# Sample states and SSD output projection of a decoder step: two blocks merged into one

## What is computed

```python
# per sequence; h is the state [group 4, head-in-group 8, 64, 128]; cum = cumsum(dt * a_neg)
y = y + einsum('blgn,bgjpn->blgjp', cc, h) * exp(cum)[..., None]      # read of the carried state
h = h * exp(last)[..., None, None] + einsum('bsgn,bsgjp->bgjpn', bc, xdt * w_s)   # its update
...
y = y + d_skip * xs
gated = y * silu(z)                                                    # [tokens, 2048]
gated = gated * rsqrt(mean(gated**2 over each of 4 groups of 512) + 1e-6)
mixer_out = (gated * norm_w) @ w_out                                   # w_out [2048, 1024]
```

## Time and profile before

| | |
|---|---|
| median of 3 runs | 1516.48 us (1514.39 to 1521.14) |
| the profiled execution, its own time | 1507.41 us |
| its span, first to last instruction | 1505.6 us |
| granted TensorE clock, mean | 0.849 of 2.4 GHz |
| TensorE matmul busy | 1281.0 us (85%) |
| VectorE busy | 459.2 us (31%) |
| ScalarE busy | 240.7 us (16%) |
| GpSimd busy | 131.3 us (9%) |

### The profile page before, as it was taken

How to read it: one execution, slowest core, us unless ns; L and a number is a source line. 1 busy time by engine, 2 the same in 40 slices (tenths; PEclk the granted TensorE clock), 3 DMA queues, 4 the chain that set the end, 5 groups by cost and what they waited for, 6 DMA issues and landing times. The chain is left out here.

```text
span 1505.6 us, 14743 instructions
## 1 busy us (share of the span) xinstructions
PE 1281.0 (85%) x5148; PEld 696.3 (46%) x5148; DVE 459.2 (31%) x1209; ACT 240.7 (16%) x570; POOL 131.3 (9%) x191
## 2 busy tenths in 40 slices
PE   7999946678996999999888489779998989998881
PEld 4777744466663335333333245545565353333330
DVE  0057745442435005322211432222110054122114
ACT  0101122110002003111111312321111032111111
POOL 0000012421000000111110000000000001111100
PEclk9999978655556998999999699597766989999996
DMA  5333450002322247799998540423524277999983
GB/s 231 120 112 111 174 226 0 29 1 83 113 111 102 84 168 287 273 424 422 423 422 368 213 201 0 132 58 96 141 79 188 91 290 295 426 423 422 424 341 114
DMA packets 54798, 309.34 MB, mean 205 GB/s; under 512 B 12818, under 2 KB 17810, under 8 KB 33362
## 3 DMA queue, kind: packets, MB, share of 16 engines
q1 hardware_dynamic: 44786, 295.42, 49.7%
q0 software_dynamic: 9216, 10.51, 2.0%
q10 hardware_dynamic: 736, 2.62, 0.6%
HBM read 300.61 MB, written 30.97 MB: 220 GB/s over the span
## 5 line engine op out<-in xcount | busy, mean ns | idle before, releaser
L1098 PE MATMUL ps<-ring,xsT 128*64 128x512 f32 x704 | 165.7, 625 | 28.1 <-DMA ring<-in_experts 23.6
L302 PE MATMUL ps<-XT,ring 128*128 128x320 f32 x640 | 175.4, 438 | 11.2 <-DMA ring<-in_w_in 11.2
L302 PEld LDWEIGHTS ps<-XT,ring 128*128 128x128 f32 x640 | 123.2, 193 | 62.9 <-issue 13.2
L1098 PEld LDWEIGHTS ps<-ring,xsT 128*64 128x64 f32 x704 | 56.7, 143 | 134.2 <-issue 127.7
L1420 DVE TENSOR_TENSOR work<-work,ps 128x256 f32<-128x256 f32 x32 | 13.5, 420 | 271.7 <-ACT work L1178 271.7
L822 PE MATMUL ps<-ring,zT 128*128 128x512 f32 (+1 forms) x192 | 87.8, 605 | 0.0
L1125 PE MATMUL ps<-ring,hT 128*64 128x512 f32 x352 | 80.4, 598 | 2.2 <-DVE hT L1425 1.7
L1098 PE MATMUL ps<-hi,xsT 128*64 128x512 f32 x320 | 70.9, 595 | 5.5 <-DMA hi<-in_experts 5.5
L1024 PE MATMUL ps<-C 128*128 128x512 f32 x124 | 68.8, 672 | 0.0
L1230 POOL DMA_INDIRECT y_dram<-ys,index x32 | 32.2, 1007 | 377.5 <-DVE ys L1431 377.5
L1222 POOL DMA_INDIRECT XT<-x_dram,index x32 | 32.7, 1020 | 351.4 <-DVE index L1366 319.7
(11 more groups left out here) (292 smaller groups left out, 1657.1 us busy)
## 6 DMA issues: line engine op xcount, KB each, us to landing
ring<-in_experts SPq DMA_DIRECT2D x40, 2048.0 KB, 25.9
ring<-in_experts SPq DMA_DIRECT2D x52, 1024.0 KB, 24.6
hi<-in_experts SPq DMA_DIRECT2D x20, 2048.0 KB, 25.7
ring<-in_w_in SPq DMA_DIRECT2D x10, 2048.0 KB, 7.7
hi<-in_experts SPq DMA_DIRECT2D x20, 1024.0 KB, 31.0
ring<-in_latent SPq DMA_DIRECT2D x48, 256.0 KB, 2.9
ring<-in_w_out SPq DMA_DIRECT2D x4, 2048.0 KB, 12.8
ring<-in_state SPq DMA_DIRECT2D x4, 1024.0 KB, 6.9
```

What stands on the lines that cost most here:

```text
L302: mm = pe.matmul(ps[:, q, 0:TOK], ring[:, u, k * 512 + q * P:k * 512 + (q + 1) * P], XT[:, k, :], start=(k == 0), stop=(k == KD - 1))
L1098: mm = pe.matmul(ps[e * SLOTS:(e + 1) * SLOTS, GU[p], :].rearrange("p (g f) -> p g f", g=2), xsT[:, p, k, e * SLOTS:(e + 1) * SLOTS], w[:, ...
```

## The change

`sample_states` and `out_projection` become one block, `states_and_output`.

- Samples are taken in four pairs: sample i of the first half and sample i of the second, so that a pair has rows 0 to 31 and rows 32 to 63 of the 64. States are loaded and stored in that order.
- State read: C, zeroed outside its own sample, is the stationary operand (32 columns) and the state moves (512 columns). The four groups write four 32-partition strips of one PSUM bank; the samples of a half accumulate. exp(cum) is applied afterwards on VectorE (`ecS`), the result is transposed (`turn_reads`) and added to `xbcT`. Chunk 2 no longer makes exp(cum) per unit on ScalarE nor the product on GpSimd.
- State update: one matmul for each sample of a pair and group, with 32 rows, on row strips 0 and 32 of the array, into banks 6 and 7.
- Norm and projection of the 256 prompt columns start at once, without the samples; an update of a pair and group stands between two channel blocks. The sample rows have their own norm and are projected last, the two column halves of the output on the two halves of the PSUM partitions; ScalarE copies one half to its place.
- `wout_used` is set by the sample rows' matmuls, so by the last part of the block. SP issues the state outputs of the last pair before the first expert.

```diff
-                            for b in range(4):
-                                sp.dma_start(h0[b], a["state"][b]).then_inc(state_in[b], 16)
+                            for b, n in enumerate((0, 4, 1, 5)):
+                                sp.dma_start(h0[b], a["state"][n]).then_inc(state_in[b], 16)
...
                     for u in range(UNITS):
-                        if c:
+                        if carried:
                             act.wait_ge(seg_in, u + 1)
...
+                @block.sync
+                def _(sp):
                     load_router(sp, 0)
                     for i in range(4):
+                        if i == 3:
+                            sp.wait_ge(y_turned, 1)
+                            sp.dma_start(lnp[:, :, :], a["ln"][0]).then_inc(ln_in, 16)
+                        for half in range(2):
+                            n, b = batch(i, half)
+                            sp.wait_ge(updated, 8 * i + 7 + half)
+                            sp.dma_start(o["ssds"][n], h0[b]).then_inc(state_out, 16)
+                        if i < 2:
+                            sp.wait_ge(state_out, 32 * (i + 1))
+                            for half in range(2):
+                                n, b = batch(i + 2, half)
+                                sp.dma_start(h0[b], a["state"][n]).then_inc(state_in[b], 16)
+                        if i == 2:
+                            sp.wait_ge(state_out, 32 * (i + 1))
+                            sp.dma_start(X[:, :, :], a["x"]).then_inc(x_in, 16)
+                    sp.wait_ge(wout_used, 1)
+                    first_expert(sp, 0, 0)
+                    sp.wait_ge(wout_used, 2)
+                    first_expert(sp, 0, 1)
+                    sp.wait_ge(state_out, 128)
+                    sp.wait_ge(wout_used, 3)
+                    first_expert(sp, 0, 2)
+                    sp.wait_ge(wout_used, 4)
+                    first_expert(sp, 0, 3)
...
+                    def read_states(i):
+                        for half in range(2):
+                            n, b = batch(i, half)
+                            pe.wait_ge(state_in[b], 16 * (i // 2 + 1))
+                            for g in range(GROUPS):
+                                mm = pe.matmul(ps[32 * g:32 * g + 32, YB[half], :], Cm[:, g, half, 32 * i:32 * i + 32],
+                                               h0[b][:, g * 512:(g + 1) * 512], start=(i == 0), stop=(i == 3))
+                            mm.then_inc(read_done, 1)
...
+                    def prompts(blk):
                         pe.wait_ge(wout_in[blk // 4], 16)
                         pe.wait_ge(scaled, blk + 1)
+                        at = (blk % 4) * D
+                        for t in range(2):
                             for n in range(2):
+                                pe.matmul(ps[:, 2 * t + n, :], zT[:, blk, OFF[t]:OFF[t] + P],
+                                          ring[:, blk // 4, at + n * 512:at + (n + 1) * 512], start=(blk == 0), stop=(blk == ZB - 1))
+
+                    def update(i, g):
+                        if i or g:
+                            pe.wait_ge(updated, 8 * i + 2 * g)
+                        for half in range(2):
+                            rows = slice(32 * half, 32 * half + 32)
+                            pe.matmul(ps[:, UP[half], :], Bm[rows, i, g * STATE:(g + 1) * STATE],
+                                      xdtw[rows, g * 512:(g + 1) * 512], start=True, stop=True).then_inc(up_done, 1)
...
+                    def samples(blk):
+                        pe.wait_ge(scaled_s, blk + 1)
+                        at = (blk % 4) * D
+                        for n in range(2):
+                            mm = pe.matmul(ps[64 * n:64 * n + 64, SB, :], zT[:, blk, SAMPLE],
+                                           ring[:, blk // 4, at + n * 512:at + (n + 1) * 512], start=(blk == 0), stop=(blk == ZB - 1))
                         if blk % 4 == 3:
                             mm.then_inc(wout_used, 1)
...
+                    for g in range(GROUPS):
+                        squares(g)
+                    pe.wait_ge(masked, GROUPS)
+                    pe.wait_ge(ec_done, 1)
+                    read_states(0)
+                    read_states(1)
+                    for blk in range(ZB):
+                        if blk % 4 == 0 and blk >= 8:
+                            read_states(blk // 4)
+                        prompts(blk)
+                        if blk == 0:
+                            pe.wait_ge(std_done, GROUPS)
+                            pe.wait_ge(bm_done, 4)
+                        if blk < 12:
+                            update(*divmod(blk, 4))
+                        elif blk == 12:
+                            turn_reads()
+                        elif blk < 15:
+                            update(3, blk - 13)
+                    sample_squares()
+                    update(3, 2)
+                    for blk in range(4):
+                        samples(blk)
+                    update(3, 3)
+                    for blk in range(4, ZB):
+                        samples(blk)
...
+                    act.wait_ge(stds_done, 1)
+                    act.wait_ge(wout_used, 4)
+                    act.activation(ps[0:64, SB + 1, :], ps[64:P, SB, :], ACT.Copy).then_inc(split_done, 1)
...
+                    scale(0)
+                    decay(0, 0)
+                    decay(0, 1)
+                    scale(1)
+                    add_update(0, 0)
+                    scale(2)
+                    add_update(0, 1)
+                    scale(3)
+                    add_update(0, 2)
+                    add_update(0, 3)
+                    for i in (1, 2):
+                        decay(i, 0)
+                        decay(i, 1)
+                        for g in range(GROUPS):
+                            add_update(i, g)
...
+                    decay(3, 1)
+                    add_update(3, 0)
+                    add_update(3, 1)
+                    v.wait_ge(stds_done, 1)
+                    v.reciprocal(rstdS[:, :, :], rstdS[:, :, :]).then_inc(rstds_done, 1)
+                    v.wait_ge(rstds_done, 1)
+                    for blk in range(ZB):
+                        x = zT[:, blk, SAMPLE]
+                        v.scalar_tensor_tensor(out=x, in0=x, scalar=normw[:, blk:blk + 1], in1=rstdS[:, blk // 4, :],
+                                               op0=ALU.mult, op1=ALU.mult).then_inc(scaled_s, 1)
+                    add_update(3, 2)
+                    add_update(3, 3)
```

More of the change, by code:

```diff
@@ L757, in out_projection @@
-        def out_projection():
-            with ExitStack() as st:
-                s = phase_semaphores(st)
-                sq = buf(st, "sq", [P, 2, 4, TOK])
-                rstd = h1[:, 0:2 * TOK].rearrange("p (b t) -> p b t", b=2)
-                gate_done, sq_done, ms_done, std_done, rstd_done, scaled = map(
-                    s, ["gate_done", "sq_done", "ms_done", "std_done", "rstd_done", "scaled"])
-                wout_used = s("wout_used")
-                block = st.enter_context(nc.Block())
-                ms = [6, 7]
+                Cm = buf(st, "Cm", [P, GROUPS, 2, 4 * 40])
@@ L770, in _, with batch @@
+                block = st.enter_context(nc.Block())
+                YB, UP, SB = (4, 5), (6, 7), 4
+                def batch(i, half):
+                    return 4 * half + i, 2 * (i % 2) + half
                 @block.sync
@@ L806, in _ @@
                 @block.tensor
                 def _(pe):
-                    for g in range(GROUPS):
+                    def read_states(i):
[6 more added lines that the diff above has]
+                            mm.then_inc(read_done, 1)
@@ L809, in _, with squares @@
+                    def squares(g):
                         pe.wait_ge(sq_done, g + 1)
@@ L812, in _ @@
                         for i in range(4):
-                            mm = pe.matmul(ps[:, ms[g % 2], 0:TOK], const("ones"), sq[:, g % 2, i, :],
+                            mm = pe.matmul(ps[:, UP[g % 2], 0:SEQ], const("ones"), sq[:, g % 2, i, :],
                                            start=(i == 0), stop=(i == 3))
                         mm.then_inc(ms_done, 1)
-                    for blk in range(ZB):
+                    def prompts(blk):
                         pe.wait_ge(wout_in[blk // 4], 16)
@@ new lines, in update, with turn_reads @@
+                    def update(i, g):
[5 more added lines that the diff above has]
+                                      xdtw[rows, g * 512:(g + 1) * 512], start=True, stop=True).then_inc(up_done, 1)
+                    def turn_reads():
+                        for half in range(2):
+                            pe.wait_ge(y_copied, half + 1)
+                            for j in range(4):
+                                tr = pe.transpose(ps[:, YB[half], j * P:(j + 1) * P], yS[:, half, j * P:(j + 1) * P], ident)
+                        tr.then_inc(y_turned, 1)
```

(16 more changed lines are left out.)

204 lines of the change are left out of this document (93 added, 111 removed).

## The result

The changed kernel takes 1406.66 us in the median (4 runs, 1405.45 to 1410.55), the kernel before 1515.43 in the same comparison. The ratio is 0.9301, 95% interval 0.9262 to 0.9340: 108.8 us less. The forecast was 1413.0 with a range of 1394 to 1446. The profiled execution took 1410.55, the highest of the four, with a span of 1408.7.

The account below looks back on a forecast made before the run. TensorE bounds the whole part, at half clock in the sample states. Terms of -105.0 + 1 + 1 - 1 + 6 = -98.0 us gave 1409.4 from the profiled 1507.41, 1418.5 by the median; forecast 1413, range 1394 to 1446.

Parts of the forecast that it names:

- Start of the block: From the end of chunk 2 to the first state reads: reads begin at 353 us, bounds 350 and 358.
- Reads: State reads in the block: records in twos, 6.9 us for the first reads and 6.9 for pairs 2 and 3.
- Updates and shape changes: State updates in the block: two row strips share a step, 13.8 us (27.5 if not); changes of shape 6.5.
- Tail: End of the block: sample squares 3.5 us, waits 1.6 and 2.2, sample rows 13.8, copy and block change 2.0.
- What had to stay hidden: In the block, VectorE's work and state-buffer transfers lie beside TensorE's path; 1 us of stall booked for each.
- Chunk 2: Chunk before the block: ScalarE's exp and GpSimd's product lie beside its pace; gain 1 us (0 to 3).
- Late expert loads: Behind the block: the expert layer's first gather meets busy queues, costing 6 us (0 to 9.4), not won back.
- 1: Packed forms overlap less, or gather pays in full: updates +13.7, reads +13.8, gather +3.4 us; 1425 to 1447; chance 0.25.
- 2: Better than the sum: reads in fours -7, clean start -3, no gather delay -6 us; 1397; chance 0.12.
- 3: The clock stays at 1.2 GHz in the block: 1516 us, no change; chance 0.02.
- 4: The low clock lasts on into the expert layer: slower, 1531 us; chance 0.02.
- 5: The merge gains nothing, since each wait became another; chance 0.01.

Follow-up runs that it names:

- one_col_strip: Changed kernel with the state reads of all four groups writing partitions 0 to 31, after two matmuls that fill the banks: 1433.2 us (one run).
- one_row_strip: Changed kernel with both matmuls of an update on rows 0 to 31, one row strip: 1416.3 us (one run).
- squares_first: Changed kernel with the samples' sums of squares taken before prompt block 15 instead of after it: 1405.08 us.
- apart: Changed kernel with all reads and updates of the sample states first, then all 16 prompt blocks: 1448.36 us, ratio to the kernel before 0.9523.
- warm: Changed kernel with eight more idle matmuls behind the slot map of layer 0, in the wait for the gather: 1399.5 us (one run).
- hold5: Changed kernel with layer 0's load of expert 5 (3 MB) issued only after the first row gather landed: 1403.38 us, ratio to the kernel before 0.9252.
- both: Changed kernel with the edits of squares_first and hold5 together: 1399.98 us, ratio to the kernel before 0.9238.
- hold45: Changed kernel with layer 0's loads of experts 4 and 5 (6 MB) both waiting for the first gather: 1412.58 us, ratio to the kernel before 0.9329.
- before_full_rows: Kernel before with the sample-state updates on all 128 rows, zero weights in the added rows: 1482.21 us, ratio to the kernel before 0.9803.

## Why the prediction was right, and which sizes were off

The result lies in the range, 6 us under the forecast, and the mechanisms were the ones named. But errors partly cancel: the block came out cheaper than the sum, and what follows dearer.

*Start of the block.* Reads forecast at 353, measured at 352.52. That closeness is luck. Chunks 0 and 1 scatter from execution to execution, and chunk 2 began 3.6 us later than in the profile before (303.83 against 300.23). From the end of chunk 2 to the first read 14.3 us were forecast, and it was 12.1. The clock rose as it did before, in the squares.

*Reads.* This is the term of the block that was mis-sized most: 6.9 us for pairs 0 and 1 and 6.9 for the others, against 3.6 (352.52 to 356.09) and 3.7. They go in fours; one_col_strip shows it. That is 6.5 of the 11.0 us by which the block was shorter than forecast: from chunk 2's end to the expert layer 117.4 (340.42 to 457.79) against 128.4.

*Updates and shape changes.* Block and update 4.64 forecast, 4.69 measured. Row strips overlap, as chosen; one_row_strip prices the other bound at 12.4 (13.7 forecast).

*Transposes.* 1.8 forecast for 16 records; a transpose turned out to be one record, not two: 8 in 0.9 us.

*Tail.* Forecast: squares 3.5, waits 1.6 and 2.2, sample rows 13.8, end 2.0. Measured: 3.6; 1.6 and none; 5.3 and 10.5; 1.3. The dip of the clock in the first sample blocks (0.79) had not been forecast; squares_first shows that this dip and the first wait cost 3.4 us. Without the dip the second wait is 0.48 us (apart), not 2.2: the 16 scalings took 3.2 us and not 4.5. With it the wait is none.

*What had to stay hidden did.* After pair 0 the states go out at 375.7 and the next loads are issued at 382.1; the reads that need them come at 393.6. No read waited for a DMA. VectorE never held TensorE before the tail; the booked 1 + 1 us were not needed.

*Chunk 2.* 1 us forecast. From its first transpose to its last VectorE instruction it took 38.5 us before and 36.6 after (303.83 to 340.42): 1.9 less.

*Late expert loads.* The chain was the one forecast: backlog, slow gather, late product, and a stream that can't make it up. Its size was forecast at 6, with 9.4 as the most, and is 12.1 (A 303.3 against 291.2). The gather's own part was 6.5. The rest was not in the sum: the clock fell in the wait, so that the transposes took 0.9 us more and the product 2.3 more (warm gives 3.2 back), and 1.6 us more passed before the gather's issue. These make 11.2; the last 0.9 stays open. The DMA engines ran on to 500.3 and were then mostly idle until 510.2:

```profile
490.70:500.30 9.60, 2.82 (x7) 0.95 (x5) 0.04 (x1) 0.00 (x0) 2.21 (x2) 0.91 0.99 417
500.30:510.20 9.90, 7.88 (x26) 3.71 (x28) 7.21 (x15) 1.51 (x4) 0.99 (x1) 0.57 0.29 108
```

*The total.* By its own time the sum gave 1409.4 and the profiled execution took 1410.55. That closeness is luck in good part. Against the sum the block is 11.0 us shorter, chunk 2 0.9 shorter than booked, and the two booked stalls of 1 us are absent; A is 6.1 longer. The 3.6 us before chunk 2 and 5.3 from the attention on (647.6 us; 642.3 before, 642.9 in the second profile of the changed kernel) are scatter, which nothing in the sum foresaw, and they close the gap.

*Rivals.* 1 fell on overlap; its gather part held in kind, though the landing took 6.5 us more and not 9.4. Its parts add up to 13.7 + 13.8 + 3.4 over 1413, so to 1444 and not 1447. 2 was right on the reads, and on 2 of the 3 us of a clean start, but not on the gather. 3 and 4, the low clock, did not come; apart shows how near it lies: with waits and no prompt blocks between them the same updates run at the low clock. 5 fell.

## What to carry to other kernels

Before counting instructions, look at the granted clock of the stretch: a stage that TensorE fills at half clock can gain twice from being mixed with full-array work, once by the overlap and once by the clock, as it did here. Small operands pay if they are laid on separate strips of the array, even in runs of four records, and a long independent stream between them hides the hand-offs. When a block gets shorter, add up the transfers that used to lie beside it: what SP issued in its last 67 us (505 to 572 before) now stands before the next stage's first small, urgent transfer, and it can be worth holding back some of them: here 4.5 us by stage for one load of 3 MB, not resolved in whole runs.

## What the runs showed of the hardware

- Zeros raised the clock. The same records with 64 more rows of zero weights took the clock from 0.50 to 0.71 and 0.81 and the whole kernel from 1511.9 to 1482.2 us. So filling rows that would be idle can pay, even with zeros.
- Four column strips shared steps fully: 0.88 us against 3.46 for eight records.
- Short waits can be dear: 3.85 us without matmuls (hold5) and 3.92 (both) were followed by products of 9.82 and 9.70 us in place of 7.09. How dear a wait is varies: behind 0.85 us the product took 7.09 in hold45 and 8.49 in before_full_rows.
- The clock of stages with light TensorE work comes back at different times in different executions of the same code. These are stretches of the prompt attention, first of the kernel before, then of the changed one; line by line they hold about the same work:

```profile
960.00:970.00 10.00, 7.17 (x28) 6.13 (x29) 2.42 (x11) 3.08 (x11) 0.00 (x0) 0.50 0.55 157
970.00:980.00 10.00, 7.20 (x29) 4.36 (x28) 2.47 (x8) 3.02 (x9) 0.00 (x0) 0.86 0.45 126
```

```profile
858.00:868.00 10.00, 7.38 (x29) 6.26 (x30) 2.20 (x10) 3.29 (x12) 0.00 (x0) 0.50 0.60 175
868.00:878.00 10.00, 7.21 (x19) 4.20 (x18) 2.46 (x8) 2.04 (x7) 0.00 (x0) 0.50 0.42 122
878.00:888.00 10.00, 7.14 (x35) 5.12 (x34) 2.54 (x8) 3.06 (x9) 0.00 (x0) 0.85 0.60 176
```

One stretch of 10 us more at the low level, some 3 us in the end; in the second profile of the changed kernel this lag is absent. What sets the moment stays open.
